# The first memory tile of the S5 layer multiplied at the end of the GLA layer, half of it on each side of the transposes

## What is computed

```python
mem_n = rms_norm_2(mem, mem_norm_w)                     # 256 memory rows
for i in range(2):                                      # 0: GLA layer, 1: S5 layer
    h = rms_norm_2(x, norm_w[i])
    seq_out, z, xq = gla_branch(...) if i == 0 else s5_branch(...)   # both start with h @ w_in
    k, v = split(mem_n @ w_kv[i])                       # does not depend on x
    xa = softmax(xq @ k.T / 16) @ v                     # 4 heads of 256
    x = x + (concat(seq_out, xa) * silu(z)) @ w_out[i]
return rms_norm_2(x, final_norm_w)
```

## Time and profile before

| | us |
|---|---|
| median of 3 runs | 1638.78 (1637.18 to 1639.89) |
| the profiled execution, whole | 1638.86 |
| its span, first to last instruction | 1637.1 |
| TensorE busy | 1564.2 (96%) |
| VectorE busy | 519.2 (32%) |
| ScalarE busy | 287.0 (18%) |
| GpSimd busy | 74.8 (5%) |
| mean granted clock of TensorE | 0.984 |

### The profile page before, as it was taken

How to read it: one execution, slowest core, us unless ns; L and a number is a source line. 1 busy time by engine, 2 the same in 40 slices (tenths; PEclk the granted TensorE clock), 3 DMA queues, 4 the chain that set the end, 5 groups by cost and what they waited for, 6 DMA issues and landing times. The chain is left out here.

```text
span 1637.1 us, 21537 instructions
## 1 busy us (share of the span) xinstructions
PE 1564.2 (96%) x8781; PEld 930.2 (57%) x8781; DVE 519.2 (32%) x1080; ACT 287.0 (18%) x548; POOL 74.8 (5%) x109
## 2 busy tenths in 40 slices
PE   5999999899999999995999999998999999899997
PEld 2475654344434444432445588554888887588743
DVE  2444323111111111113210211122788888620000
ACT  2222101111111112111111020101222222320000
POOL 0000000000000000000000000001121221000000
PEclk9999999999999999998899999998999999999999
DMA  9444738799999999997142144234354443333440
GB/s 403 182 155 158 297 141 346 299 422 422 421 422 422 422 422 422 422 422 300 69 154 104 52 155 154 103 136 150 130 180 143 146 174 133 116 119 139 154 154 26
DMA packets 53740, 375.98 MB, mean 230 GB/s; under 512 B 7200, under 2 KB 18080, under 8 KB 19120
## 3 DMA queue, kind: packets, MB, share of 16 engines
q1 hardware_dynamic: 53392, 374.02, 57.7%
q10 hardware_dynamic: 288, 1.11, 0.2%
HBM read 373.99 MB, written 1.11 MB: 229 GB/s over the span
## 5 line engine op out<-in xcount | busy, mean ns | idle before, releaser
L1228 PE MATMUL ps<-ring,x_gathered 128*64 128x512 f32 x1024 | 225.2, 592 | 0.9 <-DVE x_gathered L1296 0.9
L1950 PE MATMUL ps<-hT,ring 128*128 128x256 f32 x768 | 172.4, 383 | 1.9 <-PEq L113 1.9
L1416 PE MATMUL ps<-ring,zT 128*128 128x512 f32 x384 | 165.6, 592 | 0.0
L1950 PEld LDWEIGHTS ps<-hT,ring 128*128 128x128 f32 x768 | 145.3, 192 | 23.5 <-issue 4.3
L1228 PEld LDWEIGHTS ps<-ring,x_gathered 128*64 128x64 f32 x1024 | 73.5, 137 | 146.6 <-issue 146.6
L1305 DVE TENSOR_TENSOR act_slots<-gate,ps 64x512 f32<-64x512 f32 x32 | 22.1, 690 | 378.6 <-ACT gate L1267 378.6
L1416 PEld LDWEIGHTS ps<-ring,zT 128*128 128x128 f32 x384 | 72.8, 190 | 89.9 <-issue 89.7
L1251 PE MATMUL ps<-ring,act_turned 128*64 128x512 f32 x512 | 116.9, 598 | 0.0
L1532 PE MATMUL ps<-hT,ring 128*128 128x256 f32 x512 | 111.9, 380 | 0.0
L2160 PE MATMUL ps<-uT,ring 128*128 128x256 f32 x512 | 111.0, 379 | 0.0
L1532 PEld LDWEIGHTS ps<-hT,ring 128*128 128x128 f32 x512 | 96.8, 190 | 16.0 <-issue 3.1
(11 more groups left out here) (466 smaller groups left out, 1604.8 us busy)
## 6 DMA issues: line engine op xcount, KB each, us to landing
ring<-in_experts SPq DMA_DIRECT2D x192, 1024.0 KB, 15.7
ring<-in_weights SPq DMA_DIRECT2D x75, 2048.0 KB, 8.1
b_raw<-in_s_b SPq DMA_DIRECT2D x16, 128.0 KB, 7.2
s_a_rows<-s_ab_rows SPq DMA_DIRECT2D x64, 32.0 KB, 6.5
c_raw<-in_s_c SPq DMA_DIRECT2D x16, 128.0 KB, 6.2
b_by_state<-in_s_b_by_state SPq DMA_DIRECT2D x16, 128.0 KB, 2.0
x<-in_x ACTq DMA_DIRECT2D x1, 1024.0 KB, 5.3
mix_room<-in_mem SPq DMA_DIRECT2D x1, 1024.0 KB, 15.1
```

The costliest lines, as they stand in the source:

```text
L1228: last = pe.matmul(h_ps[rows, :], xg[:, f, :], w[:, kk, m, :], start=(f == 0), stop=(f == KD - 1))
L1416: last = pe.matmul(self.bank(n, t), self.zT[:, 8 * kb + kk, t * P:(t + 1) * P], w[:, kk, :], start=(first and kk == 0), stop=(self.ends(i) ...
L1950: last = pe.matmul(out[:, f, :], w[:, kk, (2 * h + f) * P:(2 * h + f + 1) * P], rhs[:, kk, :], start=(kk == 0), stop=(kk == KD - 1))
```

## The change

The keys' first weight tile (halves 24 and 25 of before) becomes the tile in front of the S5 layer's w_in tiles, and is multiplied in the GLA layer by `keys_half`: half 0 into bank 0 between the last tile of the output projection and the transposes, half 1 into bank 1 behind the transposes. ScalarE copies both to `kmT` behind its squares. Half 0 waits for the landed tile and for two of VectorE's residual additions. The stage of the GLA layer now loads one tile more (`stream` to `T_S5_SCAN`), and its last load waits for `keys_half(1)`.

The scan has 15 tiles, 30 halves. Halves 24 and 25 are now the second tile of the keys, 26 to 29 the values. By `starts` the steps begin with halves 2, 4, 6, 8, 9, 11, 13, 15, 16, 18, 20, 22, 23, 25, 27 and 29: steps 3, 7, 11 and 15 have one half, all others two. In steps 4 to 6 and 12 to 14 the first half is the odd one, the second half of a tile.

```diff
 T_S5 = T_GLA_OUT + 6
-T_GLU = T_S5 + 16
+T_S5_SCAN = T_S5 + 1
+T_GLU = T_S5_SCAN + 15
@@ stage_gla_layer
+        keys_done, keys_out = k.sem("s5_keys_half_done"), k.sem("s5_keys_out")
...
-                stream(k, sp, T_GLA, T_S5)
+                stream(k, sp, T_GLA, T_S5_SCAN)
                 sp.wait_ge(ab_out, 16)
...
+                def keys_half(i):
+
+                    out, w = k.ps[:, i, :].rearrange("p (f t) -> p f t", f=2), k.slot(T_S5)
+                    for f in range(2):
+                        for kk in range(KD):
+                            last = pe.matmul(out[:, f, :], w[:, kk, (2 * i + f) * P:(2 * i + f + 1) * P], k.memT[:, kk, :],
+                                             start=(kk == 0), stop=(kk == KD - 1))
+                    return last
...
                 out.pe_tile(pe, 4)
                 out.pe_tile(pe, 5)
+                k.wait_tile(pe, T_S5)
+                pe.wait_ge(out.added, 2)
+                keys_half(0).then_inc(keys_done, 1)
                 pe.wait_ge(ab_copied, 1)
                 pe.wait_ge(s5_scaled, TT)
                 turn(k, pe, xn, KD, fm(hi), s5_turned)
+                keys_half(1).then_inc(k.tile_done, 1)
...
                 for n in range(2):
                     out.act_squares(act, n)
+                for i, (sem, value) in enumerate(((keys_done, 1), (k.tile_done, T_S5 + 1))):
+                    act.wait_ge(sem, value)
+                    act.activation(kmT[:, 2 * i:2 * i + 2, :], k.ps[:, i, :].rearrange("p (f t) -> p f t", f=2),
+                                   ACT.Copy).then_inc(keys_out, 1)
@@ stage_s5_scan
-        halves_of = [[2 * q + 2, 2 * q + 3] for q in range(14)] + [[30], [31]]
+        starts = [2 + 7 * (q // 4) + 2 * (q % 4) for q in range(17)]
+        halves_of = [list(range(starts[q], starts[q + 1])) for q in range(16)]
...
                 def load_tile(m):
-                    sp.wait_ge(k.tile_done, T_S5 + m - (RING - 1))
-                    sp.dma_start(k.ring[:, (T_S5 + m) % RING, :], k.dram["weights"][T_S5 + m]
-                                 ).then_inc(k.landed[(T_S5 + m) % RING], 16)
+                    sp.wait_ge(k.tile_done, T_S5_SCAN + m - (RING - 1))
+                    sp.dma_start(k.ring[:, (T_S5_SCAN + m) % RING, :], k.dram["weights"][T_S5_SCAN + m]
+                                 ).then_inc(k.landed[(T_S5_SCAN + m) % RING], 16)
@@ kernel (order of the weight tiles)
-        wide(g["s5_w_in_2"][0]), kv[1], wide(g["s5_w_glu_2"][0]),
+        kv[1][:1], wide(g["s5_w_in_2"][0]), kv[1][1:], wide(g["s5_w_glu_2"][0]),
```

More of the change, by code:

```diff
@@ L1866, in stage_s5_scan @@
         dsts = [a["uT"][:, 4 * m:4 * m + 4, :] for m in range(4)] + [a["zT"][:, 4 * m:4 * m + 4, :] for m in range(6)]
-        dsts += [a["xqT"][:, 4 * m:4 * m + 4, :] for m in range(2)] + [a["kmT"][:, 4 * m:4 * m + 4, :] for m in range(2)]
+        dsts += [a["xqT"][:, 4 * m:4 * m + 4, :] for m in range(2)] + [a["kmT"][:, 4:8, :]]
         dsts += [a["vm"][:, :, m * 512:(m + 1) * 512] for m in range(2)]
         n_half = 2 * len(dsts)
-        halves_of = [[2 * q + 2, 2 * q + 3] for q in range(14)] + [[30], [31]]
+        starts = [2 + 7 * (q // 4) + 2 * (q % 4) for q in range(17)]
+        halves_of = [list(range(starts[q], starts[q + 1])) for q in range(16)]
         def half_bank(i):
             bank = k.ps[:, 6 + i % 2, :]
-            return bank if i >= 28 else bank.rearrange("p (f t) -> p f t", f=2)
+            return bank if i >= 26 else bank.rearrange("p (f t) -> p f t", f=2)
         with k.nc.Block() as block:
@@ L1935, in half @@
                 def half(i):
-                    m, h = T_S5 + i // 2, i % 2
+                    m, h = T_S5_SCAN + i // 2, i % 2
                     if h == 0:
@@ L1942, in half @@
                     for kk in range(KD):
-                        if i >= 28:
+                        if i >= 26:
                             last = pe.matmul(out, k.memT[:, kk, h * P:(h + 1) * P], w[:, kk, :],
                                              start=(kk == 0), stop=(kk == KD - 1))
-                    if i < 28:
+                    if i < 26:
                         rhs = k.hT if i < 24 else k.memT
@@ L2026, in take @@
                 def take(i):
-                    act.wait_ge(k.tile_done if i % 2 else half_done, T_S5 + i // 2 + 1 if i % 2 else i // 2 + 1)
+                    act.wait_ge(k.tile_done if i % 2 else half_done, T_S5_SCAN + i // 2 + 1 if i % 2 else i // 2 + 1)
                     d = dsts[i // 2]
-                    d = d[:, i % 2, :] if i >= 28 else d[:, 2 * (i % 2):2 * (i % 2) + 2, :]
+                    d = d[:, i % 2, :] if i >= 26 else d[:, 2 * (i % 2):2 * (i % 2) + 2, :]
                     act.activation(d, half_bank(i), ACT.Copy).then_inc(half_out, 1)
```

## The result

The changed kernel takes 1643.53 us, median of 7 runs (1641.78 to 1646.6), the kernel before 1638.86 in runs beside it (1635.54 to 1641.13): ratio 1.0033, 95% interval 1.0020 to 1.0045. By the ratio it is slower by 5.4 us (0.0033 x 1638.86), by the two medians by 4.7; the forecast was 5.8.

What follows compares the result with a forecast made beforehand. The prediction took TensorE, busy for 96% of 1637.1 us, to bound the kernel, with about 2.7 us of slack per scan step. Its terms, 7.81 - 1.41 - 0.90 + 0.30 = +5.80 us, gave 1644.7 us, range 1639.5 to 1648.

Steps and rivals of the forecast that it cites:

- The end of the GLA layer: Half 0 partly hidden in idle time, quicker turns, half 1 exposed: the scan's first matmul 7.81 us later.
- First two halves of the scan: At the scan's start, the clock stays up, so these take 14.20 us instead of 15.61: -1.41.
- Scan steps 3, 7, 11: With one half each takes 15.62 us instead of 17.01, the half behind 8.20 instead of 7.11: -0.30 each, together -0.90.
- The end of the scan: From the start of step 14 to the last y, 25.11 us instead of 24.81: +0.30.
- Queues: At the scan's start, small loads queue behind a 2 MB tile, hidden with 3 us to spare: no cost.
- rival C: At the GLA layer's end, turns run at the lower clock, 3.65 us, 1.74 more: 1646.4 us; chance 0.04.
- Rival A: The clock holds in the scan's one-half steps, 2.35 us less for each of three: -1.25, 1637.6 us; chance 0.11.
- Rival B: One-half scan steps take TensorE's 10.1 us, if VectorE is done after 8.8: 19.8 us less, 1624.9; chance 0.04.

Runs made afterwards that it cites:

- e7_half0_alone: The kernel before with only half 0 added as extra work ahead of the transposes, the scan keeping its 32 halves; 1639.66 us, ratio 1.0008.
- e6_numbers_early_before: The kernel before with ScalarE's angle numbers made a step earlier, ahead of the copy of the step's last half; 1636.48 us, ratio 0.9985.
- e5_fill_half: The changed kernel with 16 small unused matmuls in TensorE's idle time of scan steps 3, 7 and 11, ahead of y; 1635.81 us, 0.9984 of the kernel before.
- e9_burst_moved: e4_numbers_early with GpSimd making C of step q only once VectorE has finished step q - 1; 1624.67 us, 0.9915 of the kernel before.
- e4_numbers_early: The changed kernel with ScalarE's angle numbers made a step earlier, ahead of the copy of the step's last half; 1630.69 us, 0.9958 of the kernel before.
- e10_burst_moved_before: The kernel before with both reorderings of e9_burst_moved, on ScalarE and GpSimd; 1637.46 us, ratio 0.9991.

## Why the prediction was right, point by point

- **The end of the GLA layer**, forecast +7.81: +7.49. The chain was as predicted, half 0, turns of 1.91, half 1, copy, stage change. Half 0 and the turns were each 0.2 us shorter to the next start than forecast and the copy began without a lag of 0.2; the change of stage took 1.23 us from the end of the copy and not 1.01.
- **First two halves of the scan**, forecast -1.41: -1.62. The clock held through 1.88 us of idle (e7_half0_alone, with 2.99, shows that it might not have).
- **Scan steps 3, 7, 11**, forecast 15.62 us each: 15.63, 15.63 and 15.62, with a fall of the clock in every one. The halves behind them cost +1.40, +1.51 and +1.52 (the three steps behind step 3 took 52.43 us and those behind step 7 52.54, where three of 17.01 are 51.03; steps 12 and 13 took 35.54, where two are 34.02), where the forecast had +1.09 from the one row. This term was too small by 1.2 us in all, for two reasons. It compared 8.20 us, which in the last step run to the skip product, with 7.11, which run to the B products; to the skip product an undisturbed half takes 6.97 (1417.12 to 1424.09 in the changed kernel), so the row itself says +1.23. And it took the length of the slow stretch from a single fall; how far the lower clock reaches into the next half differs from fall to fall.
- **The end of the scan**, forecast +0.30: 24.89 against 24.81, +0.08. The last half took 6.97 and not 7.11 to the skip product, the same reading as above, and step 14 took 16.93.
- **Queues**, forecast nothing: VectorE was done 3.4 us before the B products; forecast 3.
- Sum: +5.80 forecast, 7.49 - 1.62 + 0.29 + 0.08 = +6.24 by these terms (the scan steps are 3 x -1.38 + 4.43 = +0.29). That the sum came so near is in part luck: three terms were too high by 0.75 us together and one too low by 1.2. The mechanism was right in all of them.
- **The turns at the lower clock** (rival C): the turns took 1.91 us between the two halves at a granted clock of 1.00, and 3.65 where they followed an idle time. By the rule of the Trainium skill (TensorE: Matmul & The Clock Gate, Part 4: PE-mode transpose) the full clock does not engage for transposes; the measurement decides against it as a statement on their speed. In e6_numbers_early_before the clock even came back to 1.00 behind an idle time with nothing run since but the turns, as the two windows above show.
- **Rival A**, that the clock holds: it did not, and e5_fill_half shows its price, 7.9 us where the forecast had 7.05. **Rival B** was right in its price and wrong in its condition, and e9_burst_moved met the condition by other edits: its trace is 19.1 us below the changed kernel's, where the price was 19.8. What it called "no reason for less" was the order of two other engines, which this change leaves as it is.

## What to carry to other kernels

Work taken out of a step gains only down to the next engine's chain: read in the trace when the other engines' results of that step are ready, counted from its start, and look for a step that is already as the change would make the others. If TensorE must wait a few microseconds at such a place, the wait can cost twice, by itself and by the half-speed matmuls behind it. First let the slower chain loose (here the order of two operations on ScalarE and one wait on GpSimd), then move the work, and look once more at the last step, where a shorter one can run into the same chain.

## What the runs showed of the hardware

- The length of an idle time alone did not tell whether the clock falls. It fell with 1.60 us of idle in e4_numbers_early and held with 1.26 and 2.15 in the same kernel; it fell with 2.54 in e10_burst_moved_before and 2.99 in e7_half0_alone, and held with 1.88 at the stage change. In the scan the idle time stands behind the short products of B and of the skip matrix (1.66 us of them), at the stage change of the changed kernel behind a half tile; whether that decides it, no run shows. The windows of e4_numbers_early, ahead of and behind two of these idles (stretch, length, busy, granted clock, DMA):

```profile
1218.90:1220.50 1.60, 0.01 (x1) 1.00 0.24 75
1220.90:1224.30 3.40, 3.40 (x37) 0.54 0.34 90
...
1346.20:1348.40 2.20, 0.05 (x2) 1.00 0.35 117
1348.40:1352.00 3.60, 3.60 (x44) 1.00 0.25 74
```

- A matmul of 128 columns in float32 took 0.22 us, so 32 of them, 7.15 us, were as long as a half tile of 16 matmuls of 256 columns (7.1 us): the time goes by the columns that pass, and the filling was twice what the idle time could take.
- From the same work, the time to the end of the last output tile differs by up to 5 us between profiles; a few microseconds between two spans say nothing until they are located.
